# Two-layer token mixer on one core: the 31-tap convolution's running sum moves from SBUF to two PSUM banks, and the scan's scores, the latent norms and the value transposes move with it

## The reference

```python
proj = h @ w_in                                   # 21 column tiles of 128
y_a = sc_b * depthwise_conv(sc_c * sc_h, w_sc_conv)              # 3 taps
# b: gated linear attention, forwards and backwards, with decays
o = rms(gla_scan(q, k, v, la_f, True) + flip(gla_scan(..., False)))
y_b = o * silu(gg)
# c: latent attention: rms norms of cq and ckv, two small products, rope
q_c = (rms(cq) @ w_mla_uq);  k_c, v_c = (rms(ckv) @ w_mla_ukv)
y_c = softmax(q_c k_c^T) v_c
# d: a convolution of 31 taps over 256 channels
a, gate = split(cfm_in)
u = depthwise_conv(a * sigmoid(gate), w_cfm_dw)                  # 31 taps
y_d = silu(layer_norm(u))
y = concat(rms(y_a), rms(y_b), rms(y_c), rms(y_d)) @ w_out
```

## Time and profile before

| | |
|---|---|
| median of 3 runs | 2709.87 us (2705.49 to 2710.38) |
| the profiled execution | 2707.33 us, span 2705.5 us |
| PE busy | 2544.4 us, 94% of the span |
| DVE busy | 1811.0 us, 67% |
| ACT busy | 1035.2 us, 38% |
| POOL busy | 976.6 us, 36% |
| TensorE clock granted, mean | 0.975 of 2.4 GHz |
| scan stage of the first mixer layer | 1355 to 1440 us |
| scan stage of the second | 2053 to 2138 us |

### The profile page before, as it was taken

How to read it: one execution, slowest core, us unless ns; L and a number is a source line. 1 busy time by engine, 2 the same in 40 slices (tenths; PEclk the granted TensorE clock), 3 DMA queues, 4 the chain that set the end, 5 groups by cost and what they waited for, 6 DMA issues and landing times.

```text
span 2705.5 us, 34162 instructions
## 1 busy us (share of the span) xinstructions
PE 2544.4 (94%) x11326; PEld 1934.1 (71%) x11326; DVE 1811.0 (67%) x2281; ACT 1035.2 (38%) x1631; POOL 976.6 (36%) x389
## 2 busy tenths in 40 slices
PE   8999999999999999999888889999988888899997
PEld 6676788888666688888665457787766646688876
DVE  7554872776666675486797657728579855782775
ACT  4444432222344522223533644323354354432333
POOL 2222444444200144444352124445435403344442
PEclk9999999999999999999999989999988989999999
DMA  4111232222111223222211022222322102222232
GB/s 146 63 58 48 91 103 94 95 100 89 63 55 47 82 97 106 88 93 102 73 55 40 20 67 84 98 90 93 106 68 71 51 12 63 70 96 98 85 105 74
DMA packets 61022, 212.29 MB, mean 78 GB/s; under 512 B 6912, under 2 KB 7168, under 8 KB 60800
## 3 DMA queue, kind: packets, MB, share of 16 engines
q1 hardware_dynamic: 60064, 209.60, 23.6%
q10 hardware_dynamic: 864, 1.44, 0.2%
HBM read 208.92 MB, written 2.10 MB: 78 GB/s over the span
## 4 chain that ended last, share of the span: by engine, by line
PE 72%; DVE 15%; ACT 5%; issue 5%; POOL 2%; DVEq 1%; ACTq 0%; DMA 0%; POOLq 0%; SPq 0%
PE bank_G L531 21%; PE bank_G L533 20%; PE bank_G L532 20%; POOL wlo L465 2%; DVE conv_up L929 2%; DVE mx L2544 1%; ACT whi L504 1%; PE bank_X L2132 1%; DVE prod L949 1%; PE bank_S L1527 1%; PE bank_X L1013 1%; PE bank_X L1555 1%; DVE h L784 1%; DVE h L808 1%; PE bank_O L1775 1%
## 5 line engine op out<-in xcount | busy, mean ns | idle before, releaser
L465 POOL TENSOR_TENSOR wlo<-raw,whi 128x1024 fp32r<-128x1024 f32 (+2 forms) x367 | 931.8, 2539 | 1639.1 <-ACT whi L504 1639.0
L531 PE MATMUL bank_G<-n_hi,whi 128*128 128x512 f32 x2264 | 921.5, 407 | 52.1 <-DVE n_lo L788 28.0
L533 PE MATMUL bank_G<-n_hi,wlo 128*128 128x512 f32 x2264 | 892.2, 394 | 0.0
L532 PE MATMUL bank_G<-n_lo,whi 128*128 128x512 f32 x2264 | 892.2, 394 | 0.0
L504 ACT ACTIVATE whi<-raw 128x1024 fp32r<-128x1024 f32 (+2 forms) x395 | 410.5, 1039 | 684.1 <-PE bank_G L533 682.8
L531 PEld LDWEIGHTS bank_G<-n_hi,whi 128*128 128x128 f32 x2264 | 431.4, 191 | 185.4 <-issue 58.7
L533 PEld LDWEIGHTS bank_G<-n_hi,wlo 128*128 128x128 f32 x2264 | 431.1, 190 | 93.9
L532 PEld LDWEIGHTS bank_G<-n_lo,whi 128*128 128x128 f32 x2264 | 432.5, 191 | 90.1 <-issue 6.8
L531 PE MATMUL bank_G<-a_hi,whi 128*128 128x512 f32 x704 | 276.6, 393 | 6.1 <-DVE a_lo L951 3.5
L532 PE MATMUL bank_G<-a_lo,whi 128*128 128x512 f32 x704 | 274.1, 389 | 0.0
L533 PE MATMUL bank_G<-a_hi,wlo 128*128 128x512 f32 x704 | 274.0, 389 | 0.0
(11 more groups left out here) (322 smaller groups left out, 2757.3 us busy)
## 6 DMA issues: line engine op xcount, KB each, us to landing
raw<-in_w_mix_in SPq DMA_DIRECT2D x42, 512.0 KB, 3.3
raw<-in_w_hyb_in SPq DMA_DIRECT2D x25, 512.0 KB, 3.4
raw<-in_w_diff_in SPq DMA_DIRECT2D x24, 512.0 KB, 3.3
raw<-in_w_up0a SPq DMA_DIRECT2D x22, 512.0 KB, 3.3
raw<-in_w_up0b SPq DMA_DIRECT2D x22, 512.0 KB, 3.3
raw<-in_w_up1a SPq DMA_DIRECT2D x22, 512.0 KB, 3.3
raw<-in_w_up1b SPq DMA_DIRECT2D x22, 512.0 KB, 3.3
raw<-in_w_up2a SPq DMA_DIRECT2D x22, 512.0 KB, 3.3
```

Of the source, the lines that this page charges most:

```text
L465: pool.tensor_tensor(b.wlo[:, g.slot, 0:width], b.raw[:, g.slot, 0:width], b.whi[:, g.slot, 0:width], ALU.subtract).then_inc(b.lo_ready, 1)
L531: pe.matmul(out, b.whi[:, g.slot, w], hi[:, hi_at + k, :], start=(k == 0), stop=False)
L532: pe.matmul(out, b.whi[:, g.slot, w], lo[:, lo_at + k, :], start=False, stop=False)
L533: mm = pe.matmul(out, b.wlo[:, g.slot, w], hi[:, hi_at + k, :], start=False, stop=(k == pieces - 1))
```

## The change

The sum of the long convolution is kept in the banks O0 and O1; each tap reads `cpad` in SBUF and the sum in PSUM and writes PSUM. The last tap writes its result to `mx` in SBUF. The scores of the scan use S and X in place of S and O. Since the X banks are then taken during the scan, the SUMS matmuls with ACT's work on them and the VG transposes with DVE's copies move behind the scan: behind GEMM tile 16, ahead of tile 17. UKV and UQ stand together behind tile 17. `TAPS` is dealt out anew: 11 taps (22 instructions) ahead of the first turn instead of 9 (18), 4 and 4 in turns 0 and 1 instead of 3 and 3, one in each later turn as before, 3 and the last one behind the scan instead of 8. Cut to its core:

```diff
-    posts = ([("AUP", d) for d in range(2)] + [("VG", j) for j in range(2)] + [("SUMS", d) for d in range(2)]
+    posts = ([("AUP", d) for d in range(2)] + [("SUMS", d) for d in range(2)] + [("VG", j) for j in range(2)]
...
 def scan_bank(b, n):
-    return (b.S, b.S, b.O, b.O)[n % 4][:, n % 2, :]
+    return (b.S, b.S, b.X, b.X)[n % 4][:, n % 2, :]
+
+def scan_copied_pe(pe, b, l):
+    pe.wait_ge(b.g_copy_act, SCAN_ACT * (l + 1))
+    pe.wait_ge(b.g_copy_dve, SCAN_DVE * (l + 1))
...
-TAPS = (9, 3, 3, 1, 1, 1, 1, 1, 1, 1, 4, 4)
+TAPS = (11, 4, 4, 1, 1, 1, 1, 1, 1, 1, 3)
...
 def mixer_pe(pe, b, l):
         if turn == 0:
             pe.wait_ge(b.evacuated, g0 + M_GQ + 1)
+            for d in range(2):
+                taken_out(pe, b, x_at(l, "AUP", d))
             scan_scores_pe(pe, b, l, "same")
-        if turn == 3:
-            ... transposes VG
-        if turn == 7:
-            ... ones_pe SUMS 0, SUMS 1
         scan_scores_pe(pe, b, l, level)
     tile(LATE_TILES - 3)
+    scan_copied_pe(pe, b, l)
+    pe.wait_ge(b.mla_sq, 3 * (l + 1))
+    ... ones_pe SUMS 0, SUMS 1, transposes VG
+    tile(LATE_TILES - 2)
     pe.wait_ge(b.mla_n, 3 * (l + 1))
     ... UKV
-    tile(LATE_TILES - 2)
     ... UQ
     tile(LATE_TILES - 1)
     ... rotations, VM transposes
-    pe.wait_ge(b.g_copy_act, SCAN_ACT * (l + 1))
-    pe.wait_ge(b.g_copy_dve, SCAN_DVE * (l + 1))
+    pe.wait_ge(b.cfm_u, l + 1)
...
 def mixer_act(act, b, link, l, mixw):
-        if turn == 7:
-            ... Ln and Exp of SUMS
     tile(LATE_TILES - 3)
+    ... Ln and Exp of SUMS
+    tile(LATE_TILES - 2)
     ... UKV
-    tile(LATE_TILES - 2)
...
 def mixer_dve(dve, b, link, l):
-                u = b.mx[:, M_A + j, :]
-                dve.scalar_tensor_tensor(u, b.cpad[:, j, bass.ds(i + (first + 1), T)],
-                                         v_(b, f"cfm_dw{l}", 2 * i + (2 * first + 2 + j)), u, ALU.mult,
+                dve.scalar_tensor_tensor(b.O[:, j, :], b.cpad[:, j, bass.ds(i + (first + 1), T)],
+                                         v_(b, f"cfm_dw{l}", 2 * i + (2 * first + 2 + j)), b.O[:, j, :], ALU.mult,
                                          ALU.add).then_inc(b.conv_tap[j], 1)
...
-        dve.tensor_scalar(b.mx[:, M_A + j, :], b.cpad[:, j, 0:T], v_(b, f"cfm_dw{l}", j), None,
+        dve.tensor_scalar(b.O[:, j, :], b.cpad[:, j, 0:T], v_(b, f"cfm_dw{l}", j), None,
...
-        if turn == 4:
-            ... copies of VG
-        if turn == 8:
-            ... three scalings by the latent norms
         taps(turn + 1)
     taps(10)
-    taps(11)
+    ... copies of VG, three scalings by the latent norms
+    last_tap()        # reads cpad and O, writes mx[:, M_A + j]
     dve.sem_inc(b.cfm_u, 1)
```

More of the change, by code:

```diff
@@ L2170, in mixer_pe @@
             pe.wait_ge(b.evacuated, g0 + M_GQ + 1)
+            for d in range(2):
+                taken_out(pe, b, x_at(l, "AUP", d))
             scan_scores_pe(pe, b, l, "same")
-        if turn == 3:
-            for j in range(2):
-                transpose_pe(pe, b, Index(g0 + M_GV + j), x_at(l, "VG", j), b.mx[:, M_GV + j, :])
-        if turn == 7:
-            pe.wait_ge(b.mla_sq, 3 * (l + 1))
-            ones_pe(pe, b, x_at(l, "SUMS"), "ones", [b.sq[:, 0, :]])
-            ones_pe(pe, b, x_at(l, "SUMS", 1), "ones", [b.sq[:, 1, :], b.mixed[:, 0, :]])
         scan_scores_pe(pe, b, l, level)
     tile(LATE_TILES - 3)
+    scan_copied_pe(pe, b, l)
+    pe.wait_ge(b.mla_sq, 3 * (l + 1))
+    ones_pe(pe, b, x_at(l, "SUMS"), "ones", [b.sq[:, 0, :]])
+    ones_pe(pe, b, x_at(l, "SUMS", 1), "ones", [b.sq[:, 1, :], b.mixed[:, 0, :]])
+    for j in range(2):
+        transpose_pe(pe, b, Index(g0 + M_GV + j), x_at(l, "VG", j), b.mx[:, M_GV + j, :])
+    tile(LATE_TILES - 2)
     pe.wait_ge(b.mla_n, 3 * (l + 1))
@@ L2340, in mixer_act @@
     tile(LATE_TILES - 3)
+    for d, (dst, n) in enumerate(((b.rstd, P), (b.mean, 2 * P))):
+        p = x_at(l, "SUMS", d)
+        act.wait_ge(b.posted, p.at(1))
+        act.activation(dst[:, :], b.X[:, p.slot, :], ACT.Ln, bias=b.eps2, scale=1.0 / n).then_inc(b.x_free[p.slot], 1)
+    for d, dst in enumerate((b.rstd, b.mean)):
+        taken_out(act, b, x_at(l, "SUMS", d))
+        act.activation(dst[:, :], dst[:, :], ACT.Exp, scale=-0.5).then_inc(b.mla_rs, 1)
+    tile(LATE_TILES - 2)
     for m in range(4):
@@ L2541, in taps, with last_tap @@
             for j in range(2):
-                u = b.mx[:, M_A + j, :]
                 dve.wait_ge(b.conv_tap[j], l * CFM_W + 1 + first + i)
-                dve.scalar_tensor_tensor(u, b.cpad[:, j, bass.ds(i + (first + 1), T)],
-                                         v_(b, f"cfm_dw{l}", 2 * i + (2 * first + 2 + j)), u, ALU.mult,
+                dve.scalar_tensor_tensor(b.O[:, j, :], b.cpad[:, j, bass.ds(i + (first + 1), T)],
+                                         v_(b, f"cfm_dw{l}", 2 * i + (2 * first + 2 + j)), b.O[:, j, :], ALU.mult,
                                          ALU.add).then_inc(b.conv_tap[j], 1)
+    def last_tap():
+        k = CFM_W - 1
+        assert sum(TAPS) == k - 1
+        for j in range(2):
+            dve.wait_ge(b.conv_tap[j], l * CFM_W + k)
+            dve.scalar_tensor_tensor(b.mx[:, M_A + j, :], b.cpad[:, j, k:k + T], v_(b, f"cfm_dw{l}", 2 * k + j),
+                                     b.O[:, j, :], ALU.mult, ALU.add).then_inc(b.conv_tap[j], 1)
     dve.wait_ge(b.evacuated, g0 + M_A + 2)
@@ L2561, in mixer_dve @@
             scan_mask_dve(dve, b, l, level)
-        if turn == 4:
[L2563 to L2566, removed]
-        if turn == 8:
[L2569 to L2572, removed]
         taps(turn + 1)
     taps(10)
-    taps(11)
+    for j in range(2):
+        p = x_at(l, "VG", j)
+        dve.wait_ge(b.posted, p.at(1))
+        dve.tensor_copy(b.mx[:, M_GV + j, :], b.X[:, p.slot, :]).then_inc(b.x_free[p.slot], 1)
+    for n, (tile, gain, rs) in enumerate(((M_CKV, f"g_kv{l}", b.rstd), (M_CQ, f"g_q{l}", b.mean), (M_CQ + 1, f"g_q{l}", b.mean))):
+        dve.wait_ge(b.mla_rs, 2 * l + (1 if n == 0 else 2))
+        y = b.mx[:, tile, :]
+        dve.scalar_tensor_tensor(y, y, v_(b, gain, max(n - 1, 0)), rs[:, :], ALU.mult, ALU.mult).then_inc(b.mla_n, 1)
+    last_tap()
+    for j in range(2):
+        dve.wait_ge(b.conv_tap[j], CFM_W * (l + 1))
     dve.sem_inc(b.cfm_u, 1)
```

## The result

The changed kernel takes 2688.42 us (median of 4 runs, 2687.09 to 2690.28), the kernel before 2709.09 us beside it (4 runs, 2705.49 to 2710.38). The ratio is 0.9932, 95% interval 0.992 to 0.9944: 0.7% faster. The forecast was 2701 us within 2690 to 2710; in the same terms the ratio makes 2691.4 us of the first median, 2709.87. Direction and range held, but the gain was sized at less than half: 8.9 us foreseen, 20.2 us between the two profiled executions (2707.33 and 2687.09 us). That is beyond the forecast's own range of -5.5 to -14 us; the range as a whole held only because rival (a) was counted into it.

What follows compares the result with a forecast made beforehand. PE, busy 94% of the span, was taken to lose time waiting for DVE, whose taps POOL holds. Layers of -4.9 and -4.0 us made -8.9, 2707.33 to 2698.4; with 2.5 for the median 2701 us, range 2690 to 2710.

Steps and rivals of the forecast that it cites:

- rival (a): Near levels: POOL never holds the decays, pace 6.79 us; total -17.0, with the clock kept up -20.4 us; chance 0.18.
- The tap: DVE's convolution taps: with the sum in PSUM, 0.66 us from start to start, 22 early ones ending at 1359.8.
- The wait for the second far half: Head of the scan, first layer: the half starts at 1371.0 and PE's 5.07 us wait shrinks by 2.5.
- What the head is worth: Head of the scan: shorter PE wait plus saved clock loss, -4.0 us in the first layer, -2.2 in the second.
- the same halving: Head of the scan: half the clock loss counted as saved, 1.5 us in the first layer, 0.9 in the second.
- pace of 7.6: Near levels: 7.6 us a step with decays held by POOL's split, so 38.0 us for five steps.
- estimated 3.2 us of clock loss: First layer, second far half to level 0: some 3.2 of 9.73 us put down to a granted clock of 0.67.
- The near levels: Level 0 to 5: taps no longer meet POOL but decays do; -5.2 us in the first layer, -6.1 in the second.
- Behind the scan: Behind the scan: SUMS and VG moved there plus about 0.5 us of standing still, +4.3 us in each layer.
- The limit for the early taps: Head of the scan: early taps have until 1361.5; each further 0.1 us a tap costs 2.2 us a layer.
- rival (c): Taps in PSUM stay at 1.26 us, 22 end at 1373: +8.1 and +6.7 us, 2725 us; gain gone at 0.96; chance 0.12.

Runs made afterwards that it cites:

- Experiment 5: The kernel before, with filler matmuls in PE's waits ahead of both far levels and a near one: 2708.38 us, ratio 1.0002.
- experiment 3: The changed kernel with the masks ahead of the decays in DVE's list in each near turn: 2682.42 us, ratio 0.9905 against the kernel before.
- experiment 4: The changed kernel with 30 instead of 22 tap instructions ahead of turn 2: 2694.97 us, ratio 0.9958 against the kernel before.
- experiments 8 and 9: Two fillers in each 2.6 us wait: 8 on the changed kernel with masks before decays, value product before VM transposes, 2674.83 us; 9 on the changed kernel, 2687.72 us.

## Why the prediction was right, and where it was too small

**The tap.** Right. "0.66 us from start to start" was 14.58 us for 22 (DVE's timeline after, below); the forecast was 14.5 us, to 1359.8, and they end at 1360.05. The first multiplication into PSUM takes 750 ns.

```profile
1345.47 14.58 DVE L2549 SCALAR_TENSOR_TENSOR bank_O<-cpad,vec,bank_O 128x512 f32<-128x512 f32 x22
```

**The wait for the second far half.** Right in the first layer: it starts at 1371.08 (forecast 1371.0) and PE waits 2.60 us (forecast 2.6). In the second the wait is 2.60 too.

**What the head is worth. This step failed in its size.** I put it as the part of PE's wait that goes, plus half of an estimated clock loss: -4.0 us, and for the second layer "1.3 us go with it, and 0.9 of clock by the same halving". Measured: -5.5 and -6.4. (The 0.9 stands on no row: by the same halving it would have been 1.2, half of the 2.4 us by which that stretch, 9.14 us before, is now shorter.) The second layer's visible wait was short, 3.83 us, since PE was running at a clock of 0.75 there and arrived late itself.

Experiment 5 shows, in the second layer, that DVE's list set the time up to level 1: with the clock restored the stretch is as long as before, and PE's gap is larger. Thus wait and clock loss are one budget, DVE's lateness, and a faster DVE gives back both. The head should have been sized by DVE's list, whose early taps ended at 1367.5 and now end at 1360.05, 7.5 us sooner, down to the next limit, which is ACT's copies behind tile 8.

Counted to level 1, at which PE waited for DVE in the kernel before, the first layer gained just these 7.5 us (36.88 to 29.34) and the second 9.3 (37.09 to 27.80), where the forecast, with its pace of 7.6, comes to 5.2 and 4.3. From the second far half to level 0 it takes 6.76 us (1371.08 to 1377.84) at a clock of 1.00:

```profile
1371.10:1377.80 6.70, 6.70 (x40) 5.15 (x40) 5.00 (x10) 3.01 (x5) 2.71 (x2) 1.00 0.23 78
```

Before, it was 9.73 us at 0.67. So 3.0 of the estimated 3.2 us of clock loss came back in the first layer, not 1.5, though a gap of 2.6 us is still ahead of it. In the second layer it takes 6.76 us too (2057.34 to 2064.10). That the clock stays up behind a gap of 2.6 us is no rule: in the profile of experiment 3 it fell there. The changed kernel's four runs lie within 3.2 us of each other, but no run here tells what decides it.

**The near levels.** Right in mechanism: the decays meet POOL's weight split and hold the masks. DVE's timeline and then POOL's, at near turns, after:

```profile
1379.51 0.41 DVE L2082 TENSOR_TENSOR decayed<-ntmp 128x256 f32<-128x256 f32 x1
...
1386.60 2.62 DVE L2084 TENSOR_TENSOR decayed<-ntmp 128x256 f32<-128x256 f32 x1
```

```profile
1379.57 3.63 POOL L465 TENSOR_TENSOR wlo<-raw,whi 128x1024 fp32r<-128x1024 f32 x1 [1.87 <-ACT whi L504]
...
1386.34 2.60 POOL L465 TENSOR_TENSOR wlo<-raw,whi 128x1024 fp32r<-128x1024 f32 x1 [0.79 <-ACT whi L504]
```

Five steps took 37.13 us in either layer, 7.43 each, where the forecast was 7.6. The difference is the first step, which takes 6.77 us (1377.84 to 1384.61): DVE comes out of the head early enough for its decays to start at 1379.51, ahead of the split, and it is the split that takes longer (3.63 against 2.60 us). The other four take 7.25 to 7.92 us, 7.59 in the mean, each with one decay of 2.0 to 2.7 us. Rival (a) named this and applied it to every step; it happens in one of five. Its total with the clock kept up, -20.4 us, is what was measured, but not by its mechanism: the near levels gave 13.0 us, not the 19.4 it claimed. Experiment 3, where the decays no longer stand ahead of the masks, shows the pace of rival (a), 6.77.

**Behind the scan.** Right: +4.1 us in each layer, forecast +4.3. UKV waits for no norm.

**The limit for the early taps** ("until 1361.5"). Wrong by some 3.5 us, as experiment 4 shows: ACT was idle ahead of tile 8. By the same reasoning the break-even price of a tap in rival (c), 0.96 us, was too low.

**The rest, -3.6 us,** had no step in the prediction and needs none: profiles of kernels that are alike in those stretches differ by more (587.1 to 592.5 us in one of them). Which waits of 2.6 us let the clock fall differs from profile to profile (from 2053 to 2072 the changed kernel has 1.00, experiment 4 has 0.89 and experiment 3 has 0.82), and no run here tells what decides it; filling them won nothing that could be told from no change (experiments 8 and 9). The sum in PSUM with the old places of SUMS, VG and scores was not tried.

## What to carry to other kernels

When PE waits for a late engine and its clock is low in the same stretch, do not price the wait and the clock apart: compare the late engine's list, end to end, before and after, down to the next limit. Here DVE was busy for 18.5 of 19 us and set the time, and a filled gap and a full clock were worth nothing there (ratio 1.0002). A DVE accumulation that shares its stretch with POOL was no longer held once its running sum stood in PSUM (0.66 against 1.26 us a tap), but what comes behind it in DVE's list (here decays with two SBUF inputs) meets POOL instead: put what PE waits for ahead of it.

## What was not expected of the hardware

- A DVE instruction that reads and writes the same PSUM bank takes 751 ns for 128x512 in place of 742 with all three in SBUF; 116 of them lie between 725 and 765 ns, with PE writing other banks meanwhile.
- TENSOR_SCALAR of 128x512 with an SBUF input takes 750 ns into PSUM; before, into SBUF, the median was 484.
- POOL's instruction is longer as well: in the turn in which the decays start first (1379.51, the split at 1379.57), the split takes 3.63 us, against 2.39 to 2.60 in the other near turns.
- Fillers that kept the clock at 1.00 over 19 us where it had been 0.75 and 0.89 moved the time by 0.0002 [-0.0007, +0.0011] of it.
- Behind the same wait of 2.6 us the clock fell in some profiles and not in others (0.69 and 1.00 behind the second far half, first layer, experiment 3 and the changed kernel).
